# A three-block transformer kernel: another opening order, a last projection with the tokens held, and a bank of its own for half of one panel per phase

## The reference, cut to what matters

```python
def rmsnorm(x, g):                      # rows of length 1024
    return x * rsqrt(mean(x * x) + 1e-6) * g
def swiglu(x, wg, wu, wd):              # wg, wu: 1024 x 2816, wd: 2816 x 1024
    return (silu(x @ wg) * (x @ wu)) @ wd

h = concat(meta, x)                     # 272 x 1024
for i in (0, 1):
    h = h + 0.5 * rmsnorm(swiglu(rmsnorm(h, g[0]), ...), g[1])          # k = 0, 3
    h = h + rmsnorm(attention_i(rmsnorm(h, g[2])), g[3])                 # k = 1 (NA), 4 (DA)
    h = h + 0.5 * rmsnorm(swiglu(rmsnorm(h, g[4]), ...), g[5])          # k = 2, 5
x = h[16:]                              # 256 x 1024
x = x + rmsnorm(mixer(rmsnorm(x, g_pre) @ w_in) @ w_out, g_post)         # k = 6 (MIX)
u = square(relu(rmsnorm(x, g_mlp_pre) @ w_up))                          # k = 7 (MLP), 256 x 4096
return x + rmsnorm(u @ w_down, g_mlp_post)                              # w_down: 4096 x 1024
```

## Time and profile before

| what | value |
|---|---|
| median of 3 runs | 1504.67 us (1499.75 to 1506.32) |
| the profiled execution | 1505.06 us, its span 1503.3 us |
| TensorE (PE) busy in the span | 97% |
| weight loads (PEld) | 93% |
| VectorE (DVE) | 64% |
| ScalarE (ACT) | 44% |
| GpSimd (POOL) | 4% |
| granted TensorE clock, mean | 0.989 |
| DMA | 233.52 MB, mean 155 GB/s |

### The profile page before, as it was taken

How to read it: one execution, slowest core, us unless ns; L and a number is a source line. 1 busy time by engine, 2 the same in 40 slices (tenths; PEclk the granted TensorE clock), 3 DMA queues, 4 the chain that set the end, 5 groups by cost and what they waited for, 6 DMA issues and landing times.

```text
span 1503.3 us, 27117 instructions
## 1 busy us (share of the span) xinstructions
PE 1456.4 (97%) x11422; PEld 1400.4 (93%) x11422; DVE 956.0 (64%) x1229; ACT 659.1 (44%) x856; POOL 52.9 (4%) x75
## 2 busy tenths in 40 slices
PE   6999999999999999999999998999999998999998
PEld 5999999978999999999999967999999986999997
DVE  5665668566766557665558575866557757777554
ACT  4444346445544335444344355534434523534432
POOL 0000010011000000000010000000001010100000
PEclk9999999999999999999999998999999989999999
DMA  6586764512455664654564501455555630365551
GB/s 181 174 228 190 201 196 159 173 35 84 140 168 176 182 198 158 194 183 154 158 199 159 172 33 47 150 188 179 181 181 170 180 112 1 113 189 180 191 192 61
DMA packets 250779, 233.52 MB, mean 155 GB/s; under 512 B 29759, under 2 KB 249844, under 8 KB 250688
## 3 DMA queue, kind: packets, MB, share of 16 engines
q1 hardware_dynamic: 250224, 231.96, 49.7%
q10 hardware_dynamic: 464, 0.25, 0.1%
HBM read 230.99 MB, written 1.12 MB: 154 GB/s over the span
## 4 chain that ended last, share of the span: by engine, by line
PE 82%; DVE 8%; issue 4%; ACT 3%; DMA 2%; POOL 1%; SPq 0%; DVEq 0%
PE acc L594 24%; PE acc L593 24%; PE acc L595 24%; DVE h L1608 2%; DVE h L1602 1%; PE aux L760 1%; ACT w_hi L1164 1%; DVE rstd L1573 1%; DVE x_lo L1579 1%; PE acc L932 1%; PE acc L957 1%; DMA raw<-in_ffn_w_up 1%; PE aux L847 1%; PE aux L864 1%; POOL sq_sum L2285 1%
## 5 line engine op out<-in xcount | busy, mean ns | idle before, releaser
L593 PE MATMUL acc<-x_hi,w_hi 128*128 128x272 f32 (+1 forms) x2096 | 598.9, 286 | 8.7 <-DVE z L1696 6.3
L594 PE MATMUL acc<-x_lo,w_hi 128*128 128x272 f32 (+1 forms) x2096 | 599.5, 286 | 0.0
L595 PE MATMUL acc<-x_hi,w_lo 128*128 128x272 f32 (+1 forms) x2096 | 597.7, 285 | 0.0
L1568 DVE TENSOR_TENSOR w_lo<-raw,w_hi 128x2048 fp32r<-128x2048 f32 (+1 forms) x230 | 484.5, 2112 | 90.1 <-ACT w_hi L1164 89.6
L1164 ACT ACTIVATE w_hi<-raw 128x2048 fp32r<-128x2048 f32 (+3 forms) x251 | 406.7, 1627 | 137.9 <-DMA raw<-in_ffn_w_down 47.8
L593 PEld LDWEIGHTS acc<-x_hi,w_hi 128*128 128x128 f32 x2096 | 396.5, 189 | 11.8 <-issue 11.6
L595 PEld LDWEIGHTS acc<-x_hi,w_lo 128*128 128x128 f32 x2096 | 395.3, 189 | 0.0
L594 PEld LDWEIGHTS acc<-x_lo,w_hi 128*128 128x128 f32 x2096 | 395.2, 189 | 0.1
L593 PE MATMUL acc<-hid_hi,w_hi 128*128 128x272 f32 (+1 forms) x704 | 202.7, 288 | 0.0
L594 PE MATMUL acc<-hid_lo,w_hi 128*128 128x272 f32 (+1 forms) x704 | 201.7, 286 | 0.0
L595 PE MATMUL acc<-hid_hi,w_lo 128*128 128x272 f32 (+1 forms) x704 | 200.6, 285 | 0.0
(11 more groups left out here) (300 smaller groups left out, 1625.7 us busy)
## 6 DMA issues: line engine op xcount, KB each, us to landing
raw<-in_ffn_w_gate SPq DMA_DIRECT2D x44, 1024.0 KB, 5.3
raw<-in_ffn_w_up SPq DMA_DIRECT2D x44, 1024.0 KB, 5.3
raw<-in_ffn_w_down SPq DMA_DIRECT2D x32, 768.0 KB, 4.5
raw<-in_ffn_w_down SPq DMA_DIRECT2D x32, 640.0 KB, 4.2
raw<-in_w_up SPq DMA_DIRECT2D x16, 1024.0 KB, 5.3
raw<-in_w_down SPq DMA_DIRECT2D x16, 1024.0 KB, 5.0
raw<-in_na_w_qkv SPq DMA_DIRECT2D x12, 1024.0 KB, 5.2
raw<-in_da_w_qkv SPq DMA_DIRECT2D x12, 1024.0 KB, 5.2
```

Of the source, the lines that this page charges most:

```text
L593: nc.tensor.matmul(o, wh, xh, start=first, stop=False)
L594: nc.tensor.matmul(o, wh, xl, start=False, stop=False)
L595: return nc.tensor.matmul(o, wl, xh, start=False, stop=last)
L1568: nc.vector.tensor_tensor(w_lo[:, slot, w], raw[:, slot, w], w_hi[:, slot, w].bitcast(F32), ALU.subtract)\
```

## The change

Three things are changed at once.

**Opening.** x is loaded in two halves at the head of SyncE's queue; identity, gains and meta tokens move to ScalarE's queue; the tables are loaded only inside phase 0 (`tables_in`). TensorE first runs sixteen matmuls on ones (`keep_warm`). VectorE makes x_lo of chunk c-3 between the copies; its constant work moves behind panel 3 (`constants`). ScalarE makes w_hi of panel 0 after its fifth x_hi. Panel 0 is computed as three passes over the chunks, high by high first, so that w_lo of panel 0 is wanted last (`opening_panel`). Panel 2 of phase 0 also goes to aux 0 and 1. The table matmuls move behind panel 3. The sum of squares of phase 0 moves from chunk 4 to chunk 6 of panel 1. `ps_sum` moves from aux 3 to aux 2.

**Fourth panel.** For k > 0, panel 3 computes its first 128 output features into aux 3, and only its second 128 into the pair of panel 1 (`fourth_panel`); `evacuate` takes it in two instructions. In phase 14 (MLP) panels 0 and 1 are evacuated one after the other, before any work on either.

**Last projection.** A panel of w_down is now 256 rows by all 1024 columns. The tokens are held (128 at a time) and 512 weight columns stream, into the four aux banks, one for each half row of each token block: 24 matmuls of 512 columns a panel, 384 in all. In the last panel TensorE first turns `h` of token block 0 to rows, then finishes the four quarters one after another, then turns token block 1. ScalarE squares each quarter with a row sum; VectorE multiplies it by the gain and adds the row of `h`. `unscale_h` stays; `residual`, the squares per group and the sums over features are gone for k = 7.

The diff, cut to its core:

```diff
                 if second:
-                    return rows(A["w_down_2"][0])[:, k0:k0 + nk, bass.ds(i * CW, CW)]
+                    return rows(A["w_down_2"][0])[:, bass.ds(i * 8 + 2 * j, 2), :]
...
         def banks(n, i, j):
 
-            if n % 2 == 0 and n > 0 and isinstance(i, int) and (i, j) == (0, 2):
+            if n % 2 == 0 and isinstance(i, int) and (i, j) == (0, 2):
                 return aux[:, 0:2, :]
...
-                sp.dma_start(raw[:, slot, 0:nk * CW].rearrange("p (k n) -> p k n", n=CW),
+                width = D if phase_index == 2 * MLP + 1 else CW
+                sp.dma_start(raw[:, slot, 0:nk * CW].rearrange("p (k n) -> p k n", n=width),
                              source(phase_index, i, j)).then_inc(raw_full[slot], 16)
 
 
-            sp.dma_start(ident[:, :], A["ident"]).then_inc(in_full, 16)
-            sp.dma_start(gain_rows[:, :], A["norm_g"].rearrange("l j (c p) -> (l j c) p", p=P)).then_inc(in_full, 16)
-            sp.dma_start(gain_rows2[:, :], A["vectors"]).then_inc(in_full, 16)
-            sp.dma_start(x_rows[:, :, :], A["x"][0].rearrange("(t p) d -> p t d", p=P)).then_inc(in_full, 16)
-            sp.dma_start(meta_rows[:, :], A["meta_tokens"]).then_inc(in_full, 16)
+            for g in range(2):
+                sp.dma_start(x_rows[:, :, 512 * g:512 * g + 512],
+                             A["x"][0].rearrange("(t p) d -> p t d", p=P)[:, :, 512 * g:512 * g + 512]).then_inc(x_full[g], 16)
 
...
+                if n == 2 * MLP + 1:
+                    sp.wait_ge(h_ready, DC * (MIX + 2))
+                    sp.dma_start(gain_wide[:, :], A["vectors"][G_MLP_POST - 96:G_MLP_POST - 96 + DC, :]
+                                 .rearrange("c p -> (c p)").partition_broadcast(P)).then_inc(gain_full, 16)
...
+            def opening_panel():
+                for part, xs, ready in ((w_hi, x_hi, x_hi_ready), (w_hi, x_lo, x_ready), (w_lo, x_hi, None)):
+                    if part is w_lo:
+                        pe.wait_ge(w_lo_ready, 1)
+                    for k in range(DC):
+                        if ready is not None:
+                            pe.wait_ge(ready, k + 1)
+                        if ready is x_hi_ready and k == 0:
+                            pe.wait_ge(w_hi_ready, 1)
+                        for m in range(2):
+                            w = slice(k * CW + m * P, k * CW + m * P + P)
+                            mm = nc.tensor.matmul(acc[:, 0, m, 0:NT], part[:, 0, w], xs[:, k, :],
+                                                  start=ready is x_hi_ready and k == 0,
+                                                  stop=part is w_lo and k == DC - 1)
+                mm.then_inc(panel_used, 1)
+            def table_lines():
+                pe.wait_ge(tab_full, 32)
+                pe.wait_ge(sd_ready, 1)
+                nc.tensor.matmul(aux[0:8, 2, :], table[:, :], onehot[:, 0:512], start=True, stop=True)
+                nc.tensor.matmul(aux[0:8, 3, 0:line.shape[1] - 512], table[:, :], onehot[:, 512:], start=True, stop=True)\
+                    .then_inc(line_ready, 1)
+            def fourth_panel(k_, tokens):
+                ph = PHASES[2 * k_]
+                slot = (ph.p0 + 3) % SLOTS
+                pe.wait_ge(w_lo_ready, ph.p0 + 4)
+                for m, bank in enumerate((aux[:, 3, :], acc[:, 1, 1, :])):
+                    if m == 1:
+                        pe.wait_ge(acc_free, ph.a0 + 2)
+                    for k in range(DC):
+                        w = slice(k * CW + m * P, k * CW + m * P + P)
+                        mm = product(bank[:, 0:tokens], w_hi[:, slot, w], w_lo[:, slot, w], x_hi[:, k, 0:tokens],
+                                     x_lo[:, k, 0:tokens], k == 0, k == DC - 1)
+                mm.then_inc(panel_used, 1)
...
                 if k_ == 0:
-                    for j in range(4):
-                        one(0, j, free(0, j), sums if j == 1 else None,
-                            (lambda k: pe.wait_ge(x_ready, k + 1)) if j == 0 else (lambda k: None))
+                    opening_panel()
+                    for j in range(1, 4):
+                        one(0, j, None if j == 2 else free(0, j), sums if j == 1 else None, at=6)
+                    table_lines()
                 else:
                     first_panels(k_, tokens)
                     one(0, 2, ph.a0, sums, at=1)
-                    one(0, 3, ph.a0 + 2)
...
+            def row_products(slot, kk, k, t, b, first, last):
+                o = aux[:, 2 * t + b, :]
+                w = slice(D * kk + 512 * b, D * kk + 512 * b + 512)
+                tok = slice(P * t, P * t + P)
+                nc.tensor.matmul(o, mlp_hi[:, k, tok], w_hi[:, slot, w], start=first, stop=False)
+                nc.tensor.matmul(o, mlp_hi[:, k, tok], w_lo[:, slot, w], start=False, stop=False)
+                return nc.tensor.matmul(o, mlp_lo[:, k, tok], w_hi[:, slot, w], start=False, stop=last)
+            def rows_of_h(t):
+                for c in range(DC):
+                    tr = nc.tensor.transpose(acc_flat[:, 2 * t + c // 4, P * (c % 4):P * (c % 4) + P],
+                                             h[:, c, P * t:P * t + P], ident[:, :])
+                tr.then_inc(out_turned, 1)
+            def down_rows(units_before):
+                ph = PHASES[2 * MLP + 1]
+                for p in range(ph.panels):
+                    slot = (ph.p0 + p) % SLOTS
+                    last = p == ph.panels - 1
+                    pe.wait_ge(w_lo_ready, ph.p0 + p + 1)
+                    pe.wait_ge(hid_ready, units_before + p + 1)
+                    if last:
+                        pe.wait_ge(acc_free, ph.a0)
+                        pe.wait_ge(h_scaled, 4 * MLP)
+                        rows_of_h(0)
+                        for t in range(2):
+                            for b in range(2):
+                                for kk in range(2):
+                                    mm = row_products(slot, kk, 2 * p + kk, t, b, False, kk == 1)
+                                mm.then_inc(quarter_done, 1)
+                    else:
+                        for kk in range(2):
+                            for t in range(2):
+                                for b in range(2):
+                                    mm = row_products(slot, kk, 2 * p + kk, t, b, p == 0 and kk == 0, False)
+                        mm.then_inc(panel_used, 1)
+                rows_of_h(1)
...
-            pe.wait_ge(in_full, 16 * 5)
-            nc.tensor.transpose(ps_sum[:, 0:96], gain_rows[:, :], ident[0:96, 0:96])
-            nc.tensor.transpose(ps_sum[:, 96:G_COLS], gain_rows2[:, :], ident[0:G_COLS - 96, 0:G_COLS - 96])\
+            pe.wait_ge(const_ready, 1)
+            keep_warm(aux[:, 0, :], 16)
+            pe.wait_ge(in_full, 16 * 4)
+            nc.tensor.transpose(aux[:, 3, 0:96], gain_rows[:, :], ident[0:96, 0:96])
+            nc.tensor.transpose(aux[:, 3, 96:G_COLS], gain_rows2[:, :], ident[0:G_COLS - 96, 0:G_COLS - 96])\
                 .then_inc(gains_turned, 1)
             for c in range(DC):
+                if c % 4 == 0:
+                    pe.wait_ge(x_full[c // 4], 16)
                 wait(pe, h_ready, c - 2)
                 bank = aux[:, c % 3, :]
                 for t in range(2):
                     nc.tensor.transpose(bank[:, P * t:P * t + P], x_rows[:, t, P * c:P * c + P], ident[:, :])
                 nc.tensor.transpose(bank[:, NX:NT], meta_rows[:, P * c:P * c + P], ident[0:NM, 0:NM])\
                     .then_inc(x_turned, 1)
-            pe.wait_ge(tab_full, 32)
...
-            pe.wait_ge(sd_ready, 16)
...
-            def split_first(behind):
+            def split_first():
 
                 tokens = SUBS[0][3]
                 for c in range(DC):
                     high_part(0, c)
-                behind()
+                    if c == 4:
+                        first_high(0)
+                first_high(1)
                 for pair in range(4):
                     square(0, pair, h[:, 2 * pair:2 * pair + 2, 0:tokens], tokens)
...
-                    if (local + 1) % groups_of == 0 and local < last:
+                    if (local + 1) % groups_of == 0 and local < last and k < MLP:
...
+            act.dma_start(ident[:, :], A["ident"]).then_inc(in_full, 16)
+            act.dma_start(gain_rows[:, :], A["norm_g"].rearrange("l j (c p) -> (l j c) p", p=P)).then_inc(in_full, 16)
+            act.dma_start(gain_rows2[:, :], A["vectors"]).then_inc(in_full, 16)
+            act.dma_start(meta_rows[:, :], A["meta_tokens"]).then_inc(in_full, 16)
+            act.wait_ge(const_ready, 2)
+            load_table(ACT.Sqrt)
+            def tables_in():
+                act.dma_start(table[:, :], A["t5_rel_bias"]).then_inc(tab_full, 16)
...
+                act.dma_start(meta_in[:, :], A["na_meta_bias"][0]).then_inc(rpb_full, 16)
             def first_high(p):
...
                     if n == 0 and j == 0:
-                        load_table(ACT.Sqrt)
```

(65 more changed lines are left out.)

150 lines of the change are left out of this document (62 added, 88 removed).

## The result

| | median of 6 | lowest to highest | profiled execution |
|---|---|---|---|
| before | 1506.38 us | 1499.75 to 1510.13 | 1505.06, clock 0.989 |
| changed | 1489.21 us | 1484.42 to 1499.34 | 1499.34, clock 0.980 |

The ratio is 0.9898, 95% interval 0.9877 to 0.9919. By the medians the change makes the kernel 17.2 us faster, by the ratio, which weighs all executions, 15.4 (0.9898 x 1506.38 = 1491.0); 20.1 were forecast. The median lies 4.2 above the forecast 1485.0, inside the range; the time by the ratio is at the range's upper end. The profiled execution of the changed kernel is the slowest of its six, so single differences between the two profiles must be read stage by stage: the two differ by 5.7 us only.

A forecast was written before the change was run, and what follows sets the result against it. TensorE, busy for 97% of the span, was taken as the bound. Gains of 5.3 (opening), 4.5 (fourth panel), 4.2 (last projection) and 6.1 (end) sum to 20.1, so 1505.06 becomes 1485.0 us, range 1479 to 1491.

The forecast's parts named there:

- Opening, 5.3: Phase 0: earlier inputs and first product at 14.6 end panel 3 and its tables at 43.05, not 48.36: 5.3 us gained.
- rival 2: Opening gives less: panel 0 lands no earlier than 13.66 or the clock stays low 7 us; 3.3 us, total 1488; chance 0.19.
- the 4.2 allowed: Opening: us of first products assumed to run at half clock before the clock rises, half of it lost.
- Fourth panel, 4.5: Panel 3 of phases 2 to 14: evacuation waits go, limited by w_lo of panel 4; 4.5 us gained (2.5 to 9).
- Last projection, 4.2: Phase 14's last projection: 384 matmuls of 512 columns at 0.2244 us take 87.1 with transposes, not 91.3; 4.2 us gained.
- rival 1: Last projection: 512 columns run like plain 32-bit, 0.455 us a matmul, so the kernel gets slower, 1573 us; chance 0.03.
- End, 6.1: After the last product: 6.6 us remain instead of 12.7, a gain of 6.1 us (5.0 to 6.6).
- slower rival: Another name for rival 1: last projection at 0.455 us a matmul, kernel at 1573 us; chance 0.03.
- waits fully gained: Fourth panel: w_lo of panel 4 comes earlier too, so the part gives 8.7 us, total 1481; chance 0.10.
- Rivals 2 and 4: Opening gives only 3.3 us, 1488, chance 0.19; fourth panel's gain is given back wholly, 1489.5, chance 0.05.
- products farther apart than 0.23: Last projection: sign that the forecast is wrong; it expected 0.224 us between products.

The follow-up runs named there:

- e1: The changed kernel run again unedited, in rounds against the kernel before: 1488.67 us, ratio 0.9883.
- e5: The changed kernel with each half row of the last projection taken as two matmuls of 256 columns: 1489.12 us, ratio to before 0.9892.
- e2: The changed kernel with the last projection and the end as in the kernel before: 1496.95 us, ratio to before 0.9935.
- e4: The changed kernel with the opening of the kernel before (old queues, order, constants and table products): 1493.48 us, ratio to before 0.9918.
- e3: The changed kernel without the fourth panel's bank, evacuations in one piece and in the old order in phase 14: 1494.08 us, ratio to before 0.9920.
- e6: The changed kernel with the last projection's operands rounded to bfloat16 by the same splits: 1485.01 us, ratio to before 0.9848.
- e9: The changed kernel with more keep-warm matmuls where the differential and mixed attentions let the clock fall: 1483.38 us, ratio to before 0.9841.

## Why the prediction was right or wrong

- **What bounds.** Right: TensorE carries 88% of the last chain, and nearly every us gained is one in which it waited, ran at half clock or had no products left; only 0.9 came from cheaper products.
- **Opening, 5.3.** Right in the sum (5.28) and in the places: first product 14.6 forecast, 14.82 found; panel 3 waits for w_lo. Its clock did not behave as the step had it. The step let the clock be low until the products raised it; in fact it was up from 4.51 and fell at 11.34, while TensorE transposed, which rival 2 had expected. The price was smaller than that rival's: of the 6.83 us at half clock only 3.35 lay under products, against the 4.2 allowed. That the allowance covered it is luck in part. In e1, with the same transposes, the clock held, and phase 2 started 7.3 earlier than before; over the profiled executions with the new opening the gain is 3.8 to 7.3 (e5 and e1), wider than the 4.0 to 6.8 of the step. Its lower figure should read 4.3 by its own sum, 1.0 for the later landing.
- **Fourth panel, 4.5.** Right. k = 1 and 4 give 0.70 and 0.77 (0.70 forecast each), k = 6 gives 1.29 (1.3), k = 2 and 3 give 0.31 and 0.34 (0.35), k = 5 gives nothing (0.1), and the wait of phase 14 moved to w_lo of panel 4 with 3.08 from start to start, 2.96 more than without a wait (3.2). Its yield hangs on the clock as foreseen: 95.94 to 95.53 where the clock falls behind the new wait, to 94.08 where it does not (e2 and e4, with the same wait of 3.1): 0.4 or 1.9, where 0.2 or 1.9 stood. In the stages that is 3.8 or 5.3 together; e3 puts the whole part at 5.4.
- **Last projection, 4.2: the step that failed.** The step took 0.1178 for 256 columns apart into 0.1067 for columns at 2.4 GHz and 0.0111 fixed, and saved the fixed part 384 times: 384 x 0.0111 = 4.3. Columns of this four-byte type cost 0.451 ns, not 0.417, and only 0.0022 is fixed (e5), so 0.9 is saved, and 91.20 became 90.24. The rest of the step was right: nothing new gates it, a panel takes the same time from the first to the 15th. The trace of before held the answer: 272 columns take 6.00 / 48 = 0.1250 and 256 take 0.1178, so 16 columns cost 0.0072, 0.45 ns each. Two widths at one clock give the slope; one width and an assumed rate do not. The same misreading stands in rival 1, which says that 272 and 256 columns of this type run at one a cycle: by those rows they take 0.460 ns each, fixed part included, where a cycle is 0.417. The Trainium skill (TensorE: Matmul & The Clock Gate, "Wait — 56ns, not 53.3ns?") has 215.7 ns for 512 columns and 2.5 ns fixed. e6 agrees for bfloat16 with 215.9 in all; for the four-byte type the fixed 2.2 is near the rule's, but 512 columns take 233.3 here. The text weighed that rule and put it aside because 256 columns did not fit, and did not ask why they did not.
- **End, 6.1.** Right, a little low: 12.71 - 5.89 = 6.8. The block in the middle of the tail (last quarter: square, scale, reciprocal, two passes) took 3.4 from the last product to VectorE's last end, where 3.7 stood, and 2.5 followed instead of 2.9.
- **Sum.** 5.3 + 4.5 + 1.0 + 6.8 = 17.6 with the forecast 4.5, or 16.9 to 18.4 with the measured 3.8 to 5.3, against 17.2 and 17.9 measured; on the medians nothing was given back in the attentions. The range held the medians (1489.2, 1488.7) but with 2 us to spare: the 3.2 us of the failed step took the rest, and executions of a low clock in the attentions lie outside it. The slower rival (0.455 a matmul) was refuted by 0.233, and "waits fully gained" by the wait at panel 4. Rivals 2 and 4 stood at 1488 and 1489.5, nearer to the median than the forecast, but by coincidence: of the 3.3 for the opening and the nothing for the fourth panel that their sums need, the stages show 5.3 and 3.8 or more. In the profiled execution, 10 us slower than the median, the attentions were 5.3 us longer than before and the output phase of k = 3 3.8. The first goes with the clock, the second with one slow load; the forecast had neither.
- **Which text of the forecast pointed to it.** It named "products farther apart than 0.23" as what would make it wrong; they are 0.2333 apart.

## What to carry to other kernels

Take a fixed cost per instruction only from two sizes of the same instruction in one trace; if the larger size scales with the smaller, fewer and larger instructions save nothing. When a wait is taken away, compute what is late next and move that as well: here the buffer gave 0.4 to 1.9 us in its best phase, and reordering VectorE behind it gave another 3.1 to 4.6. Matmuls of little work put into the last waits before a dense stretch can repay themselves: in e9 they bought a higher mean clock and 5 to 6 us, though the stage that holds them got 1.6 us longer at full clock.

## What the runs showed of the hardware

- A matmul of four-byte operands (the reduced type) costs 0.451 ns a column and 0.0022 us fixed at a granted clock of 1.00 (256, 272 and 512 columns). One of bfloat16 and 512 columns costs 0.2159 us, against 0.2333. Loading 128 x 128 weights takes 188 and 98 ns (mean of the records in the changed kernel and in e6).
- The extra per column is gone at half clock. Before, at a granted 0.50, twelve matmuls of 272 columns lie between this row and the one at 24.78 of the earlier trace rows, 2.72 / 12 = 0.2267 us each, which is 0.833 ns a column, one per cycle of 1.2 GHz, with nothing fixed. At 1.00 it is 0.1250, not half of that. So a us of such products at half clock loses 0.45 us and not 0.5, and what sets the 0.451 does not scale with the engine's clock. What it is stays open.

```profile
22.06 0.43 PE L593 MATMUL acc<-x_hi,w_hi 128*128 128x272 f32 x1
```

- The granted clock stayed low while TensorE was recorded as busy nearly all the time with small matmuls; the ends of matmuls are modelled, so that busy is an upper figure. In the changed kernel's profile a window of the mixed sublayer has TensorE busy for 23.26 of 23.80 us, with 75 matmuls on 64 or 128 partitions and 64 to 256 columns, at 0.50 throughout:

```profile
1236.80:1260.60 23.80, 23.26 (x75) 17.55 (x75) 12.41 (x38) 4.75 (x18) 0.00 (x0) 0.50 0.00 0
```

- Behind the same wait in the same place the clock falls in one execution and not in another: 0.50 behind the 3.1 us in e1, 1.00 in e2.

```profile
1326.72:1330.13 3.41, 3.41 (x18) 3.41 (x17) 2.27 (x5) 2.43 (x2) 0.00 (x0) 0.50 0.54 185
```

```profile
1326.70:1330.10 3.40, 3.40 (x31) 3.40 (x31) 2.41 (x4) 2.32 (x2) 0.00 (x0) 1.00 0.39 134
```

- The time of one execution follows its mean granted clock: the changed kernel took 1499.34 at 0.980, 1492.40 at 0.985 and 1484.42 at 0.992, 1.1 to 1.4 us for each 0.001. The first of the three also has the slow load in it.
